# One 6 MB transfer for each expert of a mixture-of-experts layer, and a result that lags by one expert

## The chip, the cores and the metric

The kernel runs on one core of one Trainium2 chip. The metric is device time in microseconds. The time before is the median of three executions.

## The reference, cut to what matters

Two transformer blocks follow one another on 512 tokens of width 1024, all in float32. The change touches only the last part, a hierarchical mixture of 64 experts, of which each token uses two:

```python
# N_EXPERTS = 64, D_MODEL = 1024, D_FF_EXPERT = 512, MOE_TOP_K = 2
def expert_block(args):
    xblk, e = args
    hdn = jax.nn.silu(xblk @ w1[e]) * (xblk @ w3[e])
    return hdn @ w2[e]
...
yb = lax.map(expert_block, (xb, blk_e)).reshape(n_rows, d)
return jnp.zeros_like(xt).at[buf_tok].add(yb * buf_w[:, None])
```

w1 and w3 of an expert are 1024 x 512, w2 is 512 x 1024. Each is 2 MB, so an expert has 6.29 MB of weights and all 64 have 403 MB.

## The kernel before, in words

The first 1400 us compute the attention block, its dense feed-forward layer, the second block's convolution and state-space branches, and the router. The expert stage follows and is the rest of the run.

In that stage every expert gets 64 token rows, however many of them are in use. GpSimd gathers the rows of two experts at once from DRAM (`rows`, L3016 to L3022, 128 rows of 4 KB, of which the unused ones move nothing), and writes each expert's result back with a scatter (`results`, L3024 to L3029, 128 rows of 2 KB). Both use GpSimd's DMA queue, q0. During iterations 3 to 26 GpSimd also issues one small table write each (L3056 to L3059) on the same queue. The gather of pair q is issued at the top of GpSimd's iteration 2q-4, and TensorE uses it at the top of its iteration 2q-2.

The weights come on SyncE's queue, q1, one DMA for each matrix. There are nine slots of 16 KB for each partition (`ring9`, L789), each with its own semaphore. `use_order` (L797 to L804) lists the matrices in the order in which TensorE uses them. The loop at L3136 issues them in that order. Load i waits until TensorE has finished with load i-9, which is known from the PSUM bank of its last matmul: `mh` for w1 and w3, `my` for w2. A line of 16 KB for each partition is contiguous in DRAM. The last w2 comes in four parts, each with a semaphore of its own (`LAST_PARTS`).

TensorE (L1444 to L1462) does in iteration n, in this order:

- for even n `rows`: eight transposes of the next gathered pair (L1405), which VectorE scales and copies to SBUF (L2839);
- `hidden(n)`: w1 and w3 of expert n, in two halves of the array at once (L1418, L1420), 32 matmul instructions in all;
- `turn(n-1)`: four transposes of the hidden values (L1428), after ScalarE has copied them out of PSUM (L1555);
- `result(n-2)`: 16 matmul instructions with w2 (L1441), after ScalarE's silu (L2028) and VectorE's product (L2868). VectorE scales the result (L2876), and the scatter follows.

The result therefore lags by two experts. The PSUM banks are handed out by `bank_table` in the same order. A loop for experts with more than 64 tokens (`over_blocks`) stands behind the stage.

Of the kernel before, what the change touches and what calls it, by code (L numbers as in the profile page):

```python
# [7 lines left out]
F32 = mybir.dt.float32  # L8
# [13 lines left out]
NE = 64  # L22
BLK = 64
OVER = 16
# [31 lines left out]
DMA_SEMS = ["const", "in0", "in1", "in2", "in3", "param", "ol", "c_d", "nck0", "nck1", "w0", "w1", "w2", "w3", "m0", "m1", "m2", "m3", "m4",  # L56
# [10 lines left out]
LAST_PARTS = ["ymix", "x2b", "y01"]  # L67

# [114 lines left out]
def bank_table(ps):  # L183
# [174 lines left out]
    for n in range(NE + 2):  # L358
        if n < NE:
            if n % 2 == 0 and n + 2 < NE:  # L360
                gather(n // 2 + 1)
            if n < NE - 1:
                t("mh", n)
        if 1 <= n <= NE:
            t("mt", n - 1)
        if n == NE - 2:
            t("mh", NE - 1)
        if n >= 2:
            t("my", n - 2)
# [169 lines left out]
def build_program(nc, a):  # L539
    with ExitStack() as ctx:  # L540
# [5 lines left out]
        for name, off, n in [(f"r{off}", off, n) for off, n in PARTS_AT] + [("ring_r", 32768 + 2 * WC, 2 * WC)]:  # L546
            with ExitStack() as under:
                if off:
                    under.enter_context(nc.sbuf_tensor("before_" + name, [128, off], F32))
                parts[name] = under.enter_context(nc.sbuf_tensor(name, [128, n], F32R))  # L550
# [136 lines left out]
        EW = [A[:, 12288 + WC * i:12288 + WC * (i + 1)] for i in range(3)]  # L687
# [101 lines left out]
        ring9 = [(RG[:, i * WC:(i + 1) * WC], sem[f"w{i}"]) for i in range(4)] + [(A[:, 12288 + WC * i:12288 + WC * (i + 1)], sem[f"m{i}"]) for i in range(5)]  # L789
        if len(loads) % 2:  # L790
            ring9[0], ring9[1] = ring9[1], ring9[0]
        ring9 = [ring9[i] for i in (0, 1, 4, 8, 6, 3, 2, 5, 7)]
        before9 = [[ld.value for ld in loads if ld.slot is s] for _, s in ring9]
        before9 = [max(x) if x else 0 for x in before9]


        use_order = []  # L797
        for n in range(NE + 2):
            if n < NE - 1:
                use_order += [("w1", n), ("w3", n)]  # L800
            if n == NE - 2:
                use_order += [("w1", NE - 1), ("w3", NE - 1)]
            if n >= 2:
                use_order.append(("w2", n - 2))  # L804
        turn_of = {key: i for i, key in enumerate(use_order)}

        def matrix(*key):
            i = turn_of[key]
            ap, s = ring9[i % 9]
            return ap, s, before9[i % 9] + 16 * (i // 9 + 1)  # L810
# [24 lines left out]
        def pe(e):  # L835
# [609 lines left out]
            for n in range(NE + 2):  # L1445
                if n == 0:
                    hidden(0)
                if n % 2 == 0 and n + 2 < NE:
                    rows(n // 2 + 1)
                if 0 < n < NE - 1:  # L1450
                    hidden(n)
                if n == 0:
                    u = ps("ov")
                    w.wait_ge(sem["ovl"], 1)
                    w.wait_ge(u.free, u.n)
                    e.matmul(u.ap[0:1, 0:OVER], KEEP[:, 24:25], ident[:, 0:OVER], start=True, stop=True).then_inc(u.full, 1)
                if 1 <= n <= NE:
                    turn(n - 1)
                if n == NE - 2:
                    hidden(NE - 1)  # L1460
                if n >= 2:
                    result(n - 2)  # L1462

            def block(at, done):
                loop_wait(e, osem["gather"], done * 16)
                for k in range(8):
                    m = e.transpose(PS[:, 0, k * BLK:(k + 1) * BLK], OXG[:, k * 128:(k + 1) * 128], C("ident", 0, BLK)[:, 0:BLK])
                m.then_inc(osem["xt"], 1)
                loop_wait(e, osem["xtc"], done)
                loop_wait(e, osem["load"], done * 96)  # L1470
                for k in range(8):
                    e.matmul(PS[0:64, 1, :], OXT[:, k, :], cols(EW[0], 8)[:, k, :], start=k == 0, stop=k == 7)
                    m = e.matmul(PS[64:128, 1, :], OXT[:, k, :], cols(EW[1], 8)[:, k, :], start=k == 0, stop=k == 7)
                m.then_inc(osem["h"], 1)
                loop_wait(e, osem["hc"], done)
                for j in range(4):
                    m = e.transpose(PS[:, 2, j * 128:(j + 1) * 128], H13[0][:, j * 128:(j + 1) * 128], ident)
                m.then_inc(osem["ht"], 1)
                loop_wait(e, osem["mul"], done)
                for k in range(4):  # L1480
                    for hh in range(2):
                        m = e.matmul(PS[64 * hh:64 * hh + 64, 3, :], HT[0][:, k, :], cols(EW[2], 4)[:, k, 512 * hh:512 * hh + 512], start=k == 0, stop=k == 3)
                m.then_inc(osem["y"], 1)
# [44 lines left out]
        def act(e):  # L1528
# [501 lines left out]
            for n in range(NE + 1):  # L2030
                if n == 2:
# [6 lines left out]
                if n < NE:  # L2038
                    if n >= 2:
                        ut = ps("mt", n - 2)  # L2040
                        w.wait_ge(ut.full, ut.n + 1)
                    u = ps("mh", n)
                    evict(H13[n % 2].rearrange("t (k p) -> t p k", k=4), u, ACT.Copy, src=u.ap.rearrange("t (p k) -> t p k", k=4))
                if n >= 1:
                    gate_half(n - 1)
# [27 lines left out]
        def dve(e):  # L2073
# [787 lines left out]
            for n in range(NE + 2):  # L2861
                if n < NE and n % 2 == 0 and n + 2 < NE:
                    rows(n // 2 + 1)
                if 1 <= n <= NE:
                    ex = n - 1
                    u = ps("mt", ex)
                    w.wait_ge(sem["sl"], ex + 1)
                    e.tensor_tensor(HT[ex % 2], SL[ex % 2], cols(u.ap, 4)[:, :, 64:128], ALU.mult).then_inc(u.free, 1)  # L2868
                if n >= 2:
                    ex = n - 2  # L2870
                    u = ps("my", ex)
                    if ex >= 2:
                        w.wait_ge(sem[f"yo{ex % 2}"], 16 * (ex // 2))
                    w.wait_ge(sem["g2b"], 32)
                    w.wait_ge(u.full, u.n + 1)
                    e.tensor_tensor(YO[ex % 2], u.ap, G2, ALU.mult).then_inc(u.free, 1)  # L2876
# [36 lines left out]
        def pool(e):  # L2913
# [134 lines left out]
            for n in range(NE + 2):  # L3048
# [5 lines left out]
                if n >= 2:  # L3054
                    results(n - 2)
# [5 lines left out]
            def block(at, done):  # L3061
                loop_wait(e, osem["load"], done * 96)
# [8 lines left out]
        def sp(e):  # L3071
# [64 lines left out]
            for i, (what, ex) in enumerate(use_order):  # L3136
                ap, s, _ = matrix(what, ex)
# [3 lines left out]
                elif i < 9:  # L3141

                    u = ps("so" if i < 5 else "mo", 7)
                    w.wait_ge(u.full, u.n + 1)
                    if i == 4:
# [8 lines left out]
                src = a[what][ex].rearrange("(p k) n -> p k n", p=128)  # L3154
                if (what, ex) == ("w2", NE - 1):
                    for k in range(4):
                        e.dma_start(cols(ap, 4)[:, k, :], src[:, k, :]).then_inc(sem[LAST_PARTS[k - 1]] if k else s, 16)
                else:
                    e.dma_start(cols(ap, 4 if what == "w2" else 8), src).then_inc(s, 16)  # L3159

            def block(at, done):
                loop_wait(e, osem["next"], done)
                ex = e.value_load(OVI[0:1, bass.ds(at, 1)], min_val=0, max_val=NE - 1)
                for i, (name, k) in enumerate((("w1", 8), ("w3", 8), ("w2", 4))):
                    src = a[name].rearrange("x (p k) n -> x p k n", p=128)[bass.ds(ex, 1)].rearrange("x p k n -> (x p) k n")
                    e.dma_start(cols(EW[i], k), src).then_inc(osem["load"], 16)
# [91 lines left out]
def arrays(x):  # L3258
# [8 lines left out]
        "w_mix_out": x["w_mix_out_2"][0], "w1": x["w1_2"][0], "w3": x["w3_2"][0], "w2": x["w2_2"][0],  # L3267
# [23 lines left out]
```

## Time and profile before

| | |
|---|---|
| median of 3 runs | 2425.97 us (2423.55 to 2429.41) |
| span of the profiled execution | 2425.2 us |
| time of the profiled execution around its span | not given by the page; its span is 0.8 us under the median |
| TensorE busy | 2267.0 us, 93% of the span |
| DMA in the last 16 of 40 slices | 9 tenths busy or more until the last slice, 412 to 427 GB/s |
| all DMA | 598.76 MB in 175417 packets |
| queue q1 (SyncE) | 564.39 MB |
| queue q0 (GpSimd) | 8.46 MB in 10592 packets |

Each of the 40 slices of the page is 60.6 us long. The expert stage fills the last 17 of them. A TensorE that is shown as busy may still be waiting for the DMA queues in short gaps, so the stage is read from the waits and from the DMA share, not from TensorE's busy time. GB/s is what all 16 DMA engines moved together; the queue lines of the profile give each queue's packets, its bytes, and the time of its packets as a share of the time of all 16 engines.

### The profile page before, as it was taken

How to read it: one execution, taken by the hardware profiler on the slowest of the kernel's cores; microseconds unless marked ns; L12 is line 12 of the kernel's file. 1: busy time of each engine (PE TensorE's matmuls, PEld its weight loads, DVE VectorE, ACT ScalarE, POOL GpSimd, SP SyncE). 2: the span in 40 equal slices, each digit the busy share in tenths (PEclk: the TensorE clock that was granted, in tenths of full speed). 3: DMA queues.
4: the chain of work that ended last, by engine and by line, in shares of the span. 5: the costliest groups of instructions: out<-in, count | busy, mean ns of one | idle time of the engine just before them, and what ended most of it. 6: DMA issues, size and time to landing. Idle time of an engine off the chain costs nothing. (4 is left out here: it accounts for less than half of the span.)

```text
span 2425.2 us, 26229 instructions
## 1 busy us (share of the span) xinstructions
PE 2267.0 (93%) x10596; PEld 1416.4 (58%) x10596; DVE 1048.8 (43%) x1730; ACT 718.5 (30%) x1163; POOL 783.4 (32%) x491
## 2 busy tenths in 40 slices
PE   8999999999999999999999999888888888888887
PEld 6676578888887787777777873222222222322233
DVE  6666654443456999746765233111111111211112
ACT  5435643222233333557674221000000000000001
POOL 3335655545553443433336521111111011101000
PEclk9999999999999999999999999999999999999999
DMA  4222243534545243253345269999999999999996
GB/s 161 99 101 68 96 140 113 200 134 162 190 122 139 71 104 109 75 170 120 131 153 205 104 269 412 425 422 424 424 425 425 426 426 425 427 425 426 427 426 272
DMA packets 175417, 598.76 MB, mean 247 GB/s; under 512 B 18098, under 2 KB 96946, under 8 KB 149696
## 3 DMA queue, kind: packets, MB, share of 16 engines
q1 hardware_dynamic: 156000, 564.39, 59.8%
q10 hardware_dynamic: 8704, 24.22, 2.6%
q0 software_dynamic: 10592, 8.46, 1.1%
q8 instruction: 85, 1.39, 0.3%
q14 instruction: 36, 0.29, 0.0%
HBM read 593.19 MB, written 28.97 MB: 257 GB/s over the span
## 5 line engine op out<-in xcount | busy, mean ns | idle before, releaser
L2923 POOL TENSOR_TENSOR ring_r<-ring,ring_r 128x1024 fp32r<-128x1024 f32 (+2 forms) x215 | 513.3, 2393 | 650.2 <-ACT ring_r L1544 650.0
L857 PE MATMUL ps<-r,ring_r 128*128 128x512 f32 x1512 | 605.3, 400 | 3.8 <-POOL ring_r L2923 1.5
L859 PE MATMUL ps<-r,ring_r 128*128 128x512 f32 x1512 | 590.5, 391 | 0.0
L858 PE MATMUL ps<-r,ring_r 128*128 128x512 f32 x1512 | 590.1, 390 | 0.0
L1555 ACT ACTIVATE arena<-ps 128x512 f32<-128x512 f32 (+4 forms) x200 | 150.5, 761 | 1046.8 <-PE ps L1420 852.8
L1420 PE MATMUL ps<-arena 128*64 128x512 f32 x672 | 317.9, 629 | 68.7 <-DMA arena<-in_w 68.5
L1418 PE MATMUL ps<-arena 128*64 128x512 f32 x672 | 328.8, 639 | 0.9 <-DMA arena<-in_w 0.9
L1544 ACT ACTIVATE ring_r<-ring 128x1024 fp32r<-128x1024 f32 x220 | 222.8, 1015 | 351.9 <-PE ps L859 192.1
L857 PEld LDWEIGHTS ps<-r,ring_r 128*128 128x128 f32 x1512 | 282.9, 187 | 75.3 <-issue 10.5
L3028 POOL DMA_INDIRECT y_d<-arena,cbm x64 | 63.7, 995 | 805.0 <-DVE arena L2876 539.6
L858 PEld LDWEIGHTS ps<-r,ring_r 128*128 128x128 f32 x1512 | 282.9, 187 | 64.3 <-issue 5.8
L859 PEld LDWEIGHTS ps<-r,ring_r 128*128 128x128 f32 x1512 | 282.7, 187 | 62.5
L2868 DVE TENSOR_TENSOR arena<-arena,ps 128x256 f32<-128x256 f32 x64 | 27.0, 421 | 613.6 <-ACT arena L2028 613.6
L1420 PEld LDWEIGHTS ps<-arena 128*64 128x64 f32 x672 | 93.4, 144 | 249.3 <-issue 150.0
L1420 PE MATMUL ps<-ring,arena 128*64 128x512 f32 x352 | 169.1, 637 | 43.7 <-DMA ring<-in_w 43.7
L1418 PE MATMUL ps<-ring,arena 128*64 128x512 f32 x352 | 166.6, 621 | 1.1 <-DVE arena L2839 1.1
L1441 PE MATMUL ps<-ring,arena 128*64 128x512 f32 x672 | 153.5, 599 | 0.0
L2480 DVE SCALAR_TENSOR_TENSOR ps<-arena,params_sb,ps 128x512 f32<-128x512 f32 x232 | 153.1, 749 | 0.0
L1420 PEld LDWEIGHTS ps<-ring,arena 128*64 128x64 f32 x352 | 49.7, 146 | 141.5 <-issue 82.2
L1418 PEld LDWEIGHTS ps<-arena 128*64 128x64 f32 x672 | 93.4, 146 | 44.6 <-issue 39.6
L2876 DVE TENSOR_TENSOR arena<-ps,scr 128x512 f32<-128x512 f32 x64 | 44.3, 691 | 170.9 <-PE ps L1441 167.1
L1441 PEld LDWEIGHTS ps<-ring,arena 128*64 128x64 f32 x672 | 44.5, 137 | 79.0 <-issue 79.0
(377 smaller groups left out, 2550.8 us busy)
## 6 DMA issues: line engine op xcount, KB each, us to landing
arena<-in_w SPq DMA_DIRECT2D x105, 2048.0 KB, 33.7
ring<-in_w SPq DMA_DIRECT2D x86, 2048.0 KB, 37.0
ring<-in_w_ada SPq DMA_DIRECT2D x12, 2048.0 KB, 7.9
ring<-in_ffn_w_in SPq DMA_DIRECT2D x22, 1024.0 KB, 7.6
ring<-in_w_in SPq DMA_DIRECT2D x40, 512.0 KB, 6.2
ring<-in_w_in SPq DMA_DIRECT2D x8, 2048.0 KB, 9.3
ring<-in_fox_w_in SPq DMA_DIRECT2D x7, 2048.0 KB, 8.4
arena<-acs_d SPq DMA_DIRECT2D x16, 512.0 KB, 3.6
```

What stands on the lines that cost most here:

```text
L857: e.matmul(out, wh[:, k, :], X.hi[:, k0 + k, :], start=first and k == 0, stop=False)
L858: e.matmul(out, wh[:, k, :], X.lo[:, k0 + k, :], start=False, stop=False)
L859: m = e.matmul(out, wl[:, k, :], X.hi[:, k0 + k, :], start=False, stop=last and k == nk - 1)
L1418: e.matmul(u.ap[0:64], x, cols(w1, 8)[:, k, :], start=k == 0, stop=k == 7)
L1420: m = e.matmul(u.ap[64:128], x, cols(w3, 8)[:, k, :], start=k == 0, stop=k == 7)
L1441: m = e.matmul(u.ap[64 * hh:64 * hh + 64], HT[ex % 2][:, k, :], cols(w2, 4)[:, k, 512 * hh:512 * hh + 512], start=k == 0, stop=k == 3)
L1544: e.activation(GH[t], raw, ACT.Copy).then_inc(sem["gr_hi"], 1)
L1555: return e.activation(dst, u.ap if src is None else src, func, **how).then_inc(u.free, 1)
L2480: m = e.scalar_tensor_tensor(acc if i < 30 else cv[:, nt, :], u_rows[:, nt, i:i + T], PR[:, w0:w0 + 1], acc, ALU.mult, ALU.add)
L2876: e.tensor_tensor(YO[ex % 2], u.ap, G2, ALU.mult).then_inc(u.free, 1)
L2923: e.tensor_tensor(GL[t], grans[t][1], GH[t].bitcast(F32), ALU.subtract).then_inc(sem["gr_lo"], 1)
L3028: e.indirect_dma_start(a["y_d"], bass.IndirectOffsetOnAxis(ap=YROW[:, ex:ex + 1], axis=0), YO[ex % 2], None, bounds_check=4 * T - 1, oob_i ...
```

## The change

The host lays w2, w1 and w3 of an expert side by side, so that a partition's 48 KB are one contiguous line in DRAM. SBUF has three slots of 48 KB for each partition in place of nine of 16 KB, at the same addresses. Experts 9 to 60 come in one DMA of 6 MB. The load of expert n waits for `my` of expert n-3, that is, for the whole slot. The first nine matrices come singly, experts 3 to 8 and 61 to 63 come as w1 with w3 (32 KB lines) and w2 (16 KB lines).

The result of expert n-1 now stands between `hidden(n)` and `turn(n)`. ScalarE's, VectorE's and GpSimd's loops are moved by one iteration to match, and the last steps stand in a list.

```diff
+SLOT_OF = (1, 0, 2)
+PARTED = 9
+LAST_STEPS = [("mh", NE - 2), ("mt", NE - 2), ("mh", NE - 1), ("my", NE - 3), ("mt", NE - 1), ("my", NE - 2), ("my", NE - 1)]
...
+        first = [("w3", 0), ("w2", 2)]
+        for what, n in (first[::-1] if len(loads) % 2 else first) + [("w1", 0), ("w3", 1), ("w2", 1), ("w1", 1), ("w2", 0), ("w1", 2), ("w3", 2)]:
+            expert_load(n, what)
+        for n in range(3, PARTED):
+            expert_load(n, "w1", "w3")
+            if n > 3:
+                expert_load(n - 1, "w2")
+        expert_load(PARTED - 1, "w2")
+        for n in range(PARTED, NE - 3):
+            expert_load(n, "w2", "w1", "w3")
+        for n in range(NE - 3, NE):
+            expert_load(n, "w1", "w3")
+        for n in range(NE - 3, NE):
+            expert_load(n, "w2")
...
             rows(0)
-            for n in range(NE + 2):
-                if n == 0:
-                    hidden(0)
-                if n % 2 == 0 and n + 2 < NE:
+            hidden(0)
+            rows(1)
...
+            turn(0)
+            for n in range(1, NE - 2):
+                if n % 2 == 0:
                     rows(n // 2 + 1)
-                if 0 < n < NE - 1:
-                    hidden(n)
...
-                if 1 <= n <= NE:
-                    turn(n - 1)
-                if n == NE - 2:
-                    hidden(NE - 1)
-                if n >= 2:
-                    result(n - 2)
+                hidden(n)
+                result(n - 1)
+                turn(n)
+            for what, n in LAST_STEPS:
+                {"mh": hidden, "mt": turn, "my": result}[what](n)
...
                 else:
-                    kind, old = use_order[i - 9]
-                    u = ps("my" if kind == "w2" else "mh", old)
+
+                    u = ps("my" if "w2" in whats else "mh", ex - 3)
                     w.wait_ge(u.full, u.n + 1)
...
-                    e.dma_start(cols(ap, 4 if what == "w2" else 8), src).then_inc(s, 16)
+                    e.dma_start(dst, src).then_inc(done, 16)
```

The loop for overfull experts now fetches its three matrices in one DMA as well.

## Rows read from the trace of the kernel before

**Rows 1.** The page: DMA total, then the chain that ended last, by engine.

```profile
DMA packets 175417, 598.76 MB, mean 247 GB/s; under 512 B 18098, under 2 KB 96946, under 8 KB 149696
...
DMA 28%; PE 11%; issue 0%; DVE 0%; SPq 0%; ACT 0%; ACTq 0%; POOLq 0%; DVEq 0%
```

**Rows 2.** Busy time by stretch: length, PE, PEld, DVE, ACT, POOL, PEclk, DMA share, GB/s.

```profile
1450.00:1460.00 10.00, 8.40 (x43) 3.80 (x44) 8.14 (x35) 0.19 (x1) 0.99 (x1) 1.00 0.93 356
...
2000.00:2100.00 100.00, 86.08 (x373) 29.77 (x371) 16.89 (x45) 7.76 (x13) 11.14 (x11) 0.97 1.01 425
```

**Rows 3.** DMA, 2000 to 2300 us: share of 16 engines; issues, median us to landing.

```profile
DMA packets 11668, 127.74 MB, mean 426 GB/s; under 512 B 3302, under 2 KB 3302, under 8 KB 3998
...
q1 hardware_dynamic: 8616, 125.47, 98.4%
q0 software_dynamic: 3040, 2.10, 2.2%
...
y_d<-arena,cbm POOLq DMA_INDIRECT x20, 7.8
arena<-n_d,cbm POOLq DMA_INDIRECT x10, 11.9
```

**Rows 4.** DMA, 1600 to 2300 us: queue q0 and what was issued on it.

```profile
q0 software_dynamic: 7504, 5.78, 2.5%
...
y_d<-arena,cbm POOLq DMA_INDIRECT x46, 7.8
arena<-n_d,cbm POOLq DMA_INDIRECT x23, 12.0
row_d<-cbm POOLq DMA_INDIRECT x16, 7.8
```

**Rows 5.** DMA issues, 1447.4 to 1451 us: gathers while q1 stands empty.

```profile
arena<-n_d,cbm POOLq DMA_INDIRECT x2, 3.2
```

**Rows 6.** DMA issues, 2355 to 2400 us: scatters at the end.

```profile
y_d<-arena,cbm POOLq DMA_INDIRECT x5, 3.6
```

**Rows 7.** Queue q1, 600 to 700 us: packets, MB, share of 16 engines.

```profile
q1 hardware_dynamic: 13292, 16.58, 49.1%
```

**Rows 8.** Queue q1, 2389.8 to 2394.4 us.

```profile
q1 hardware_dynamic: 78, 0.27, 14.6%
```

**Rows 9.** Timeline of TensorE, two experts: start, us, line, shape, count [idle before].

```profile
1896.08 1.12 PE L1420 MATMUL ps<-arena 128*64 128x512 f32 x1 [3.21 <-DMA arena<-in_w]
...
1906.04 0.66 PE L1428 MATMUL ps<-consts_sb,arena 128*128 128x128 f32 x4
1906.62 3.66 PE L1441 MATMUL ps<-arena 128*64 128x512 f32 x16
1910.21 1.09 PE L1405 MATMUL ps<-consts_sb,arena 128*128 128x128 f32 x8
1911.23 0.64 PE L1418 MATMUL ps<-arena 128*64 128x512 f32 x1
...
1918.25 0.66 PE L1428 MATMUL ps<-consts_sb,arena 128*128 128x128 f32 x4
1918.84 3.65 PE L1441 MATMUL ps<-ring,arena 128*64 128x512 f32 x16
```

**Rows 10.** Timeline of SyncE: a load issued into an empty q1.

```profile
1403.60 0.34 SPq L3159 DMA_DIRECT2D ring<-in_w  x1
```

**Rows 11.** Busy time by stretch, the 0.9 us behind that issue.

```profile
1403.60:1404.50 0.90, 0.90 (x5) 0.74 (x5) 0.00 (x0) 0.00 (x0) 0.00 (x0) 1.00 0.00 0
```

**Rows 12.** Timeline of GpSimd: the gather behind a result's scatter.

```profile
1913.15 1.04 POOL L3021 DMA_INDIRECT arena<-n_d,cbm  x1 [0.30 <-issue]
```

**Rows 13.** Timeline of TensorE at the end: the last `hidden` and the last `result`.

```profile
2374.37 1.07 PE L1418 MATMUL ps<-ring,arena 128*64 128x512 f32 x2
...
2393.81 3.60 PE L1441 MATMUL ps<-arena 128*64 128x512 f32 x16
```

**Rows 14.** DMA issues of SyncE, 2357.6 to 2400 us: the last w2's four parts.

```profile
arena<-in_w SPq DMA_DIRECT2D x4, 512.0 KB, 34.6
```

More of the change, by code:

```diff
@@ L357, in bank_table @@
     gather(0)
-    for n in range(NE + 2):
-        if n < NE:
-            if n % 2 == 0 and n + 2 < NE:
-                gather(n // 2 + 1)
-            if n < NE - 1:
-                t("mh", n)
-        if 1 <= n <= NE:
-            t("mt", n - 1)
-        if n == NE - 2:
-            t("mh", NE - 1)
-        if n >= 2:
-            t("my", n - 2)
+    for n in range(NE - 2):
+        if n % 2 == 0:
+            gather(n // 2 + 1)
+        t("mh", n)
+        if n >= 1:
+            t("my", n - 1)
+        t("mt", n)
+    for what, n in LAST_STEPS:
+        t(what, n)
     for tt in range(4):
@@ L545, in build_program @@
         parts = {}
-        for name, off, n in [(f"r{off}", off, n) for off, n in PARTS_AT] + [("ring_r", 32768 + 2 * WC, 2 * WC)]:
+        for name, off, n in [(f"r{off}", off, n) for off, n in PARTS_AT] + [("ring_r", 32768 + 2 * WC, 2 * WC), *((f"expert{i}", 12288 + 3 * WC * i, 3 * WC) for i in range(3))]:
             with ExitStack() as under:
@@ L549, in build_program @@
                     under.enter_context(nc.sbuf_tensor("before_" + name, [128, off], F32))
-                parts[name] = under.enter_context(nc.sbuf_tensor(name, [128, n], F32R))
+                parts[name] = under.enter_context(nc.sbuf_tensor(name, [128, n], F32 if name.startswith("expert") else F32R))
         A = ctx.enter_context(nc.sbuf_tensor("arena", [128, 32768], F32))
@@ L787, in pv_done @@
             return sem["pv"], m + 1 - (m + 1) // 4
[L789 to L810, printed above, removed]
+        EX = [parts[f"expert{i}"][:, :] for i in range(3)]
@@ new lines, in build_program, with expert_load @@
+        AT = {"w2": 0, "w1": WC, "w3": 2 * WC}
+        EW2, EW1, EW3 = (EX[0][:, WC * i:WC * (i + 1)] for i in range(3))
+        expert_loads, landed, signalled = [], {}, {}
+        def expert_load(n, *whats):
+            slot = SLOT_OF[n % 3]
+            lo, hi = AT[whats[0]], AT[whats[-1]] + WC
+            name = f"xa{slot}" if whats == ("w2",) else f"xb{slot}"
+            signalled[name] = signalled.get(name, 0) + 16
+            for what in (whats if whats == ("w2",) else {*whats, "w1", "w3"}):
+                landed[what, n] = sem[name], signalled[name]
+            expert_loads.append((n, whats, EX[slot][:, lo:hi], a["wx"][n][:, lo:hi], sem[name]))
@@ L812, in build_program, with matrix @@
+        for n in range(NE - 3, NE):
+            expert_load(n, "w2")
+        def matrix(what, n):
+            return EX[SLOT_OF[n % 3]][:, AT[what]:AT[what] + WC], *landed[what, n]
         XR = Split(rawH, rawL, lambda k: lows["raw", k])
@@ L1444, in pe @@
             rows(0)
-            for n in range(NE + 2):
-                if n == 0:
-                    hidden(0)
-                if n % 2 == 0 and n + 2 < NE:
-                    rows(n // 2 + 1)
-                if 0 < n < NE - 1:
-                    hidden(n)
[L1452 to L1457, printed above, removed]
-                    turn(n - 1)
-                if n == NE - 2:
-                    hidden(NE - 1)
-                if n >= 2:
-                    result(n - 2)
+            hidden(0)
+            rows(1)
+            u = ps("ov")
+            w.wait_ge(sem["ovl"], 1)
+            w.wait_ge(u.free, u.n)
+            e.matmul(u.ap[0:1, 0:OVER], KEEP[:, 24:25], ident[:, 0:OVER], start=True, stop=True).then_inc(u.full, 1)
+            turn(0)
+            for n in range(1, NE - 2):
+                if n % 2 == 0:
+                    rows(n // 2 + 1)
+                hidden(n)
+                result(n - 1)
+                turn(n)
+            for what, n in LAST_STEPS:
+                {"mh": hidden, "mt": turn, "my": result}[what](n)
             def block(at, done):
@@ L1469, in block @@
                 loop_wait(e, osem["xtc"], done)
-                loop_wait(e, osem["load"], done * 96)
+                loop_wait(e, osem["load"], done * 64)
                 for k in range(8):
-                    e.matmul(PS[0:64, 1, :], OXT[:, k, :], cols(EW[0], 8)[:, k, :], start=k == 0, stop=k == 7)
-                    m = e.matmul(PS[64:128, 1, :], OXT[:, k, :], cols(EW[1], 8)[:, k, :], start=k == 0, stop=k == 7)
+                    e.matmul(PS[0:64, 1, :], OXT[:, k, :], cols(EW1, 8)[:, k, :], start=k == 0, stop=k == 7)
+                    m = e.matmul(PS[64:128, 1, :], OXT[:, k, :], cols(EW3, 8)[:, k, :], start=k == 0, stop=k == 7)
                 m.then_inc(osem["h"], 1)
@@ L1481, in block @@
                     for hh in range(2):
-                        m = e.matmul(PS[64 * hh:64 * hh + 64, 3, :], HT[0][:, k, :], cols(EW[2], 4)[:, k, 512 * hh:512 * hh + 512], start=k == 0, stop=k == 3)
+                        m = e.matmul(PS[64 * hh:64 * hh + 64, 3, :], HT[0][:, k, :], cols(EW2, 4)[:, k, 512 * hh:512 * hh + 512], start=k == 0, stop=k == 3)
                 m.then_inc(osem["y"], 1)
@@ L2028, in gate_half @@
                 e.activation(SL[ex % 2], cols(u.ap, 4)[:, :, 0:64], ACT.Silu).then_inc(sem["sl"], 1)
-            for n in range(NE + 1):
-                if n == 2:
+            for n in range(NE):
+                if n == 1:
                     for i in range(2):
@@ L2860, in dve, with gated, scaled @@
             e.tensor_tensor(GATE0, cols(ident, 1).broadcast_to([128, 4, 128]), WK[0].broadcast_to([128, 4, 128]), ALU.mult).then_inc(sem["wk"], 1)
-            for n in range(NE + 2):
-                if n < NE and n % 2 == 0 and n + 2 < NE:
-                    rows(n // 2 + 1)
[L2864 to L2876, printed above, removed]
+            def gated(ex):
+                u = ps("mt", ex)
+                w.wait_ge(sem["sl"], ex + 1)
+                e.tensor_tensor(HT[ex % 2], SL[ex % 2], cols(u.ap, 4)[:, :, 64:128], ALU.mult).then_inc(u.free, 1)
+            def scaled(ex):
+                u = ps("my", ex)
+                if ex >= 2:
+                    w.wait_ge(sem[f"yo{ex % 2}"], 16 * (ex // 2))
+                w.wait_ge(sem["g2b"], 32)
+                w.wait_ge(u.full, u.n + 1)
+                e.tensor_tensor(YO[ex % 2], u.ap, G2, ALU.mult).then_inc(u.free, 1)
+            for n in range(NE - 2):
+                if n % 2 == 0:
+                    rows(n // 2 + 1)
+                if n >= 1:
+                    scaled(n - 1)
+                gated(n)
+            for what, n in LAST_STEPS:
+                if what == "mt":
+                    gated(n)
+                elif what == "my":
+                    scaled(n)
             def block(at, done):
@@ L3047, in pool @@
             rows(1)
-            for n in range(NE + 2):
+            for n in range(NE + 1):
                 if n % 2 == 0 and n + 4 < NE:
@@ L3053, in pool @@
                     w.wait_ge(sem["slot"], 6)
-                if n >= 2:
-                    results(n - 2)
+                if n >= 1:
+                    results(n - 1)
                 if 3 <= n < 27:
@@ L3134, in sp @@
                     spread(p)
-            for i, (what, ex) in enumerate(use_order):
-                ap, s, _ = matrix(what, ex)
+            for i, (ex, whats, dst, src, done) in enumerate(expert_loads):
                 if i < 2:
```

32 lines of the change are left out of this document (13 added, 19 removed).

## The prediction

> **What bounds the kernel now.** I read the page's chain first: 28% of the span is DMA and 11% TensorE [rows 1]. The DMA part consists of long pieces of expert weights, so only the expert stage can give or cost much. Busy time by stretch says how full the DMA engines are there: share 1.01 and 425 GB/s from 2000 to 2100 us, with TensorE at 86 of 100 us [rows 2]. The stage is bound by bytes through full DMA engines. The queue lines give its step. q1 moves 125.47 MB in 300 us [rows 3], or 418 GB/s, so an expert's 6.29 MB take 15.04 us. Of the 11668 packets 3998 are under 8 KB, which leaves 7670 that carry 125.47 MB, 16.4 KB each: one packet for each partition's line. TensorE has slack. Behind `hidden` at 1911.23 come `turn` at 1918.25 and `result` until 1922.49 [rows 9], 11.26 us for an odd expert and 1.0 us more (L1405) for an even one, 23.5 us in a pair of 30.1.
>
> **1. Larger packets.** For one expert each of the 16 DMA engines handles 24 data packets and 3 completions now, and 8 and 1 with whole loads. That is 18 fewer. What does a packet cost beyond its bytes? q1 in [rows 3]: 0.984 x 16 x 300 us / 8616 = 548 ns at 14562 bytes. In [rows 8]: 0.146 x 16 x 4.6 / 78 = 138 ns at 3460 bytes. The line through both is 37 ns per 1000 bytes plus 9.8 ns. With [rows 7], 785.6 us / 13292 = 59 ns at 1247 bytes, it has 13.3 ns. But in the full stage the queues' shares add up to 100.8%, so packets overlap by 0.8% of 548 ns, 4.4 ns each. I take 9.8 - 4.4 = 5.4 ns. 18 x 5.4 ns x 52 whole experts = 5.1 us. The 9 experts in two loads save 9 packets each, 0.4 us. Term: -5.5 us. Bounds: 0 (lines cut up as before) and -13 us (13.3 ns with no overlap). No trace here shows a packet over 16 KB.
>
> **2. Three slots, a load released by `my` of n-3.** Let T be the landing of expert n. `hidden(n)` and `result(n-1)` take 11.26 - 0.59 (the `turn` that now comes later) = 10.7 us. Then SyncE issues load n+2; an issue into an empty queue moves nothing for 0.9 us [rows 10, 11]. First packet: T + 11.7. The engines are busy with load n+1 until T + 15.0, less what lies between a last packet and the matmul that waits for it, which no row shows (0 to 1 us). The queue stays full with 2.3 to 3.3 us to spare. The cover is thin where the clock falls. After 3.21 us of idle time `hidden` took 1896.08 to 1906.04, 9.96 us against 7.02 [rows 9]; this stretch has a mean granted clock of 0.97 [rows 2]. TensorE's idle time before an odd expert will be 15.04 - 11.26 = 3.8 us and before an even one 2.7, so the odd ones may well start at 1.2 GHz and use 2.9 us of the cover. Each then ends between 0.4 us early and 0.6 us late. For 26 such experts: 0 to +16 us. I take +2.5, since the nearer end is no wait.
>
> **3. `result` ahead of `turn`.** No instruction is added; both wait on results that are long there. `result(n-1)` needs the product of `turn(n-1)` in the step before. `turn(n)` now has ScalarE's copy (L1555) hidden behind `result(n-1)`'s 3.6 us. VectorE, ScalarE and GpSimd are idle most of the stage [rows 2]. Cost 0. PSUM: eight banks for on average four uses an expert, as before.
>
> **4. Start.** The first nine loads are again 18.9 MB, singly, behind the same waits. From 1450 on the engines are at 0.93 and above [rows 2]. Loads of experts 3 to 8 keep the old rule (w1 and w3 wait for `mh`), and TensorE, at 11.8 us an expert, is then ahead of the queue, with `my(6)` some 5 us before the load of expert 8 ends. 0 us, bounds -1 and +3.
>
> **5. End.** Now `hidden(63)` starts at 2374.37 and the last result ends at 2397.4, 23.0 us later, with four loads of w2 behind w3(63) in the queue. The last part lands at about 2357.6 + 34.6 + 2 = 2394 to 2395 [rows 13, 14], so TensorE runs on 2.5 us after it. After the change three w2 (15 us) follow, and 7.0 + 3 x 3.6 + 0.6 = 18.4 us of TensorE work: at least 3.4 us behind the last landing, 5 if a cold `hidden(61)` makes the chain late. +0.5 to +2.5, I take +1.3. The loop for overfull experts did not run and costs nothing.
>
> **Sum.** 2425.2 - 5.5 + 2.5 + 1.3 = 2423.5 us of span. The median of the runs lies 0.8 us above the span of the profile: 2424.3.
>
> **A cost on another queue.** The scatter takes 7.8 us to land in the full stage [rows 3] and 3.6 with q1 running out [rows 6]; the gather 12.0 [rows 4] and 3.2 with q1 empty [rows 5]. In the 300 us there are 20 scatters, 10 gathers and 3040 q0 packets. That is 16 x (20 x 5 + 10 x 9): 5 and 9 packets on each engine. With 46, 23 and 16 table writes of 2, it is 16 x 469 = 7504, as [rows 4] have it. A gather stands behind its scatter, 14 packets; (12.0 - 3.2) / 14 = 0.63 us each, one 16 KB packet of q1. So the engines alternate between the queues, packet by packet. With 48 KB packets every q0 packet waits some 1.85 us. In two experts q1 then offers 16 data packets and 2 completions, 18 turns, and q0 wants 19 (23 in iterations up to 26, with the table writes).
>
> The Trainium skill bears on this (DMA: Bandwidth & Descriptors, Queues, rings and completion order): an engine round-robins between its queues and drains a whole packet, typically 9 to 17 descriptors, before it switches. The alternation agrees. The size doesn't: by that rule a turn of q1 would be an engine's whole share of a 2 MB load, 4.9 us, and five turns 24 us, where a loaded scatter lands in 7.8. Its advice to coalesce transfers would by its fixed 2 us a DMA save 4 us an expert if nothing overlapped; a DMA share of 1.01 excludes that.
>
> **Rivals.**
> *B, slower: the gathers come late behind 48 KB packets.* A gather will take 3.2 + 14 x 1.85 = 29.1 us, with a table write in front 32.8. It is issued 2.9 us after its `result` (ends 1910.27, issue 1913.15 [rows 9, 12]), at T + 13.6 of odd expert n-1, 1.3 later with a table write, 2.9 later if that expert was cold. TensorE wants it at the latest 1.1 us ahead of the landing of n+2, at T + 44.0. Allowed: 27.5 to 30.4 us against 29.1, and with table writes 26.2 to 29.1 against 32.8, before any backlog. There it is late by 3.7 to 6.6 us; part 2's cover takes 0.4 to 3.3. The first dry moment of q1 lets q0 empty itself, so I let every second of the 9 table pairs pay 2.4 us, +11 us, and the later pairs nothing. 2435. It decides only when the lateness exceeds the cover; if all 9 paid in full it would be +50. For it: the turns, counted exactly. Against: only the slowest engine must keep q1 full; on engines that are ahead q0 drains freely, and small waits of part 2 drain it too.
> *C, faster: a packet's cost is not overlapped.* 18 x 9.8 ns x 52 + 0.7 = 9.9 us saved, no late issue, +0.5 at the end: 2425.2 - 9.9 + 0.5 + 0.8 = 2416.6. Against: the shares above 100%.
> *D, nothing larger moves: 48 KB lines go as three packets.* No saving, no slower q0; 2425.2 + 2.5 + 1.3 + 0.8 = 2430, or 2427 without late issues. Every line of 16 KB so far went as one packet, which speaks against it.
>
> **Chances.** A (the sum) 0.35, B 0.32, C 0.25, D 0.08. What a measurement of this kernel can tell from no change is 0.2%, 4.9 us: below 2421.1 is faster, above 2430.8 slower. A's own range is 2419 to 2430, so a little of it is faster. Faster 0.29 (C and 0.04 of A), same 0.40 (A's rest, D, a mild B), slower 0.31. Range: 2414 takes in C, nearly to the bound of part 1; 2441 takes in B with six pairs paying 3 us. A's own range is as above.
>
> **What would show it.** Packets of 48 KB in the queue lines (over 8 KB, a third as many): else D. q1 at 420 GB/s or more with share 1.01 between 1900 and 2300: part 1; the step from 15.04 to about 14.95 us. Scatters landing in 13 us or more and gathers in about 29: the turns. TensorE idle before L1405 for a DMA on n_d, with the DMA share below 1 between 1565 and 1830 us: B. Dips spread evenly with a lower granted clock: part 2. The sum is wrong if the share falls below 0.99 anywhere from 1500 to 2370, or if gathers keep to 12 us although packets are 48 KB.

## The result, and the profile after

The changed kernel takes 2452.47 us (median of four runs, 2451.15 to 2454.1), the kernel before 2427.31 beside it on the same chip: a ratio of 1.011, interval 1.0097 to 1.0122. It is slower by 1.1%, 28 us above the forecast and 11 above the range. The profiled execution spans 2451.4 us, 26.2 more than before. Times and ratios below come with runs of the kernel before on the same chip.

The page of the changed kernel: the DMA total, then the chain by engine, to be held against [rows 1], and the GB/s of the 40 slices of 61.3 us each.

```profile
GB/s 164 94 100 79 83 139 138 179 158 145 192 125 112 103 87 95 121 136 121 126 137 233 101 341 418 418 408 401 414 415 392 406 418 412 396 413 421 409 425 294
DMA packets 159145, 598.75 MB, mean 244 GB/s; under 512 B 16290, under 2 KB 95138, under 8 KB 147888
...
DMA 25%; PE 15%; issue 1%; DVE 0%; ACT 0%; POOL 0%; ACTq 0%; POOLq 0%; SPq 0%; DVEq 0%
```

The bytes are the same, the packets 16272 fewer. Nothing is lost up to slice 25. Then no slice of the expert stage but the last full one reaches 425, and in the chain TensorE has 4 points more and DMA 3 fewer. In a stage that was bound by a full queue this points at loads that wait for TensorE.

Busy time by stretch of the changed kernel (columns as in [rows 2]).

```profile
1500.00:1565.00 65.00, 58.10 (x284) 21.49 (x284) 13.32 (x34) 7.29 (x10) 14.28 (x15) 1.00 1.01 428
1565.00:1830.00 265.00, 202.48 (x900) 71.53 (x902) 38.43 (x96) 23.27 (x32) 40.09 (x40) 0.91 0.98 409
1830.00:2000.00 170.00, 140.67 (x613) 48.91 (x610) 24.61 (x61) 15.62 (x21) 17.13 (x17) 0.90 0.97 402
2000.00:2300.00 300.00, 242.12 (x1072) 85.01 (x1072) 47.46 (x120) 28.02 (x39) 30.30 (x30) 0.90 0.99 412
```

And the kernel before.

```profile
1565.00:1830.00 265.00, 231.78 (x990) 79.07 (x988) 42.27 (x107) 23.04 (x36) 43.04 (x43) 0.95 1.01 424
1830.00:2000.00 170.00, 147.84 (x628) 50.04 (x624) 25.66 (x64) 14.07 (x22) 17.18 (x17) 0.95 1.01 426
2000.00:2300.00 300.00, 259.19 (x1103) 88.15 (x1102) 46.64 (x119) 25.58 (x40) 30.38 (x30) 0.96 1.01 426
```

The loss is everywhere from the first whole loads on, with the table writes (to 1830) and without them, and with it the granted clock falls from 0.95 to 0.90. Before the first whole load is waited for (1500 to 1565) the changed kernel is the faster one, 428 against 423.

Queue q1 from 1565 to 2300 us (packets, MB, share of 16 engines), first of the kernel before, then of the changed one.

```profile
q1 hardware_dynamic: 21030, 306.31, 98.2%
```

```profile
q1 hardware_dynamic: 6737, 294.18, 95.4%
```

In 735 us the changed kernel moves 12.13 MB of weights less; at 416.7 GB/s, the rate before, that is 29.1 us. The rest of the kernel gives 3 us back, so this stretch is the whole of the loss. An expert's 6.29 MB took 15.1 us and now take 15.7.

DMA of the changed kernel, 2000 to 2300 us, beside [rows 3].

```profile
DMA packets 5680, 123.60 MB, mean 412 GB/s; under 512 B 2529, under 2 KB 2529, under 8 KB 3199
...
q1 hardware_dynamic: 2778, 121.36, 96.2%
q0 software_dynamic: 2890, 2.07, 2.1%
...
expert<-in_wx SPq DMA_DIRECT2D x19, 6144.0 KB, 19.3
y_d<-arena,cbm POOLq DMA_INDIRECT x20, 16.6
arena<-n_d,cbm POOLq DMA_INDIRECT x10, 28.5
```

5680 - 3199 = 2481 packets carry 121.36 MB, 48.9 KB each: the long lines do go as one packet. The scatter takes 16.6 us where it took 7.8, the gather 28.5 where it took 11.9; 29.1 had been forecast. Most telling is the first issue line. A load lands 19.3 us after its issue. A step, from one landing to the next, takes 14.9 us where it is shortest, so the load stands in the queue only some 4 us before its turn comes.

What TensorE waits for from 1600 to 2300 us (total, times, longest), first before, then after.

```profile
PE ps L1420 <- DMA arena<-in_w: 60.6, 22, 3.4
PE ps L1420 <- DMA ring<-in_w: 31.1, 12, 4.2
```

```profile
PE ps L1430 <- DMA expert<-in_wx: 129.2, 42, 6.2
PE ps L1417 <- DMA arena<-n_d,cbm: 8.8, 6, 3.8
```

The waits for weights grow from 91.7 to 129.2 us. Those for the gathers, rival B, are 8.8. (The total alone proves little: one experiment below has 117.4 us of them and no loss.)

Timeline of TensorE in the changed kernel, three experts (start, us, line, count, idle before). L1430 is `hidden`, L1453 `result`.

```profile
2063.22 0.64 PE L1430 MATMUL ps<-expert,arena 128*64 128x512 f32 x1 [0.57 <-DMA expert<-in_wx]
...
2070.14 3.60 PE L1453 MATMUL ps<-expert,arena 128*64 128x512 f32 x16
...
2079.84 1.12 PE L1430 MATMUL ps<-expert,arena 128*64 128x512 f32 x1 [5.51 <-DMA expert<-in_wx]
...
2088.57 3.60 PE L1453 MATMUL ps<-expert,arena 128*64 128x512 f32 x16
...
2094.73 0.64 PE L1430 MATMUL ps<-expert,arena 128*64 128x512 f32 x1 [0.85 <-DMA expert<-in_wx]
...
2111.59 1.12 PE L1430 MATMUL ps<-expert,arena 128*64 128x512 f32 x1 [5.75 <-DMA expert<-in_wx]
```

SyncE's loads in the same stretch.

```profile
2073.78 0.33 SPq L3172 DMA_DIRECT2D expert<-in_wx  x1
...
2092.21 0.33 SPq L3172 DMA_DIRECT2D expert<-in_wx  x1
```

Read the two together. The expert that landed at 2063.22 starts warm (0.64 us for its first matmul), `hidden` and `result` are through by 2073.7, and the load is issued 10.6 us after the landing and 6.1 before the next one at 2079.84. It lands 14.9 us after that one, at 2094.73: a full step. The expert that landed at 2079.84 comes after 5.51 us of idle time and starts at half the clock (1.12 us). Its `hidden` takes 8.7 us instead of 6.9, its load goes out 12.4 us after the landing and only 2.5 before 2094.73, and lands 16.9 after it, at 2111.59. That expert again finds TensorE idle for 5.75 us and slow.

The rest of the stage is less regular, but has the same two sides. From 1600 to 2300 us 18 of 45 experts start at the half clock (a first matmul of 1.1 us). Call the time from a load's issue to the landing of the load ahead of it the cover: 19 of the 51 loads that follow a whole load have less than 3 us, 15 have 5 us or more. Their mean steps are 16.2 and 15.1 us.

### The profile page after: what moved, and what is told of

Read it like the earlier page. It is cut to its first block and busy times, and to the rows that moved or that the text cites. A ratio compares the mean times of both kernels' runs of the same rounds, so it can differ in the third digit from the quotient of the medians.

```text
span 2451.4 us, 26113 instructions
## 1 busy us (share of the span) xinstructions
PE 2235.0 (91%) x10596; PEld 1410.0 (58%) x10596; DVE 1049.3 (43%) x1730; ACT 729.5 (30%) x1163; POOL 786.7 (32%) x491
## 5 line engine op out<-in xcount | busy, mean ns | idle before, releaser
L1430 PE MATMUL ps<-expert,arena 128*64 128x512 f32 x1024 | 510.9, 657 | 159.8 <-DMA expert<-in_wx 158.7
L1432 PE MATMUL ps<-expert,arena 128*64 128x512 f32 x1024 | 510.9, 657 | 0.0
L1430 PEld LDWEIGHTS ps<-expert,arena 128*64 128x64 f32 x1024 | 148.4, 151 | 474.5 <-issue 303.9
L1453 PE MATMUL ps<-expert,arena 128*64 128x512 f32 x1024 | 230.5, 592 | 1.2 <-DVE arena L2871 1.2
L1453 PEld LDWEIGHTS ps<-expert,arena 128*64 128x64 f32 x1024 | 73.1, 137 | 147.6 <-issue 147.6
L1432 PEld LDWEIGHTS ps<-expert,arena 128*64 128x64 f32 x1024 | 148.4, 151 | 0.0
L2846 DVE TENSOR_SCALAR arena<-ps,params_sb 128x128 f32<-128x128 f32 x256 | 84.5, 406 | 15.0 <-PE ps L1417 14.9
L2949 POOL TENSOR_TENSOR r<-arena,r 128x512 fp32r<-128x512 f32 x53 | 72.6, 1377 | 47.4 <-ACT r L1712 15.6
L2037 ACT ACTIVATE arena<-ps 128x256 f32<-128x256 f32 x64 | 24.6, 384 | 188.4 <-PE ps L1440 188.4
L2091 DVE RECIPROCAL scr<-scr 128x528 f32<-128x528 f32 (+1 forms) x16 | 54.4, 3402 | 42.5 <-ACT scr L1564 42.5
```

The lines of the kernel that those rows point to most:

```text
L1430: e.matmul(u.ap[0:64], x, cols(w1, 8)[:, k, :], start=k == 0, stop=k == 7)
L1432: m = e.matmul(u.ap[64:128], x, cols(w3, 8)[:, k, :], start=k == 0, stop=k == 7)
L1453: m = e.matmul(u.ap[64 * hh:64 * hh + 64], HT[ex % 2][:, k, :], cols(w2, 4)[:, k, 512 * hh:512 * hh + 512], start=k == 0, stop=k == 3)
L2846: m = e.tensor_scalar(XT[i][:, k, :], u.ap[:, 128 * j:128 * j + 128], SC2[:, k:k + 1], SH2[:, k:k + 1], ALU.mult, ALU.add)
L2949: e.tensor_tensor(dst, src, hi.bitcast(F32), ALU.subtract).then_inc(done, 1)
```

## The experiments

The theory after the result, M: loads are released too late, above all behind a slow `hidden`, and q1 runs dry for a moment. Its rival is B, the gathers that stand behind long packets. "Whole" below is a load of one expert in one DMA.

**Shorter packets, same waits.**

```diff
-                    e.dma_start(dst, src).then_inc(done, 16)
+                    for k in range(3):
+                        e.dma_start(dst[:, WC*k:WC*k+WC], src[...]).then_inc(done, 16)
```

> The changed kernel, but each whole load goes out as three DMAs of 16 KB lines, issued together behind the same wait. Two theories of the 26 us. Theory M (late release): a slot is released by the result two experts later, 10.7 us after a landing where TensorE's clock is high and some 13.5 us where it is low, and then the DMA queue runs dry for a moment. M expects no recovery: 2445 to 2456 us, and expert steps that alternate between 14.9 and 16.5 us as in the changed kernel. Theory B (48 KB packets make the gathers and scatters of the other queue late): the packets are 16 KB again, gathers land in 12 to 15 us, and the time goes back to 2425 to 2432 us.

Measured: 2464.63 us against 2424.45, ratio 1.0157 (1.0136 to 1.0178). Its DMA issues and TensorE's wait, 1600 to 2300 us.

```profile
y_d<-arena,cbm POOLq DMA_INDIRECT x44, 8.1
arena<-n_d,cbm POOLq DMA_INDIRECT x22, 12.2
```

```profile
PE ps L1430 <- DMA expert<-in_wx: 146.8, 40, 7.2
```

The gathers are as quick as before the change, TensorE waits for none, and the kernel is slower still. So B isn't what costs here. That it is 12 us slower than the change itself was not expected. Some 6 of them are the gain of the long lines, which is gone; and from 1565 to 2300 us the 16 engines stand idle for 24.2 us where it was 17.4 in the changed kernel. Why they idle longer is not shown.

**The same lines, released in two.** w1 with w3 waits for `mh` of n-3, w2 for its `my`, for every expert.

```diff
-PARTED = 9
+PARTED = 61
```

> The changed kernel, but all experts from 3 on come as experts 3 to 8 do: w1 with w3 (32 KB lines) released by the hidden step of n-3, and w2 (16 KB lines) by the result of n-3. Theory M (the whole slot is released too late to keep the queue full) expects most of the 26 us back, since two thirds of the bytes are asked for 18 us earlier: 2422 to 2434 us and steps of 15.0 us. A theory by which 48 KB packets or the larger unit are harmful in themselves expects 2430 to 2440 us, since the 32 KB packets keep half of it.

Measured over ten runs: 2425.7 us against 2425.52, ratio 1.0001 (0.9991 to 1.001). Its q1 from 1565 to 2300 us.

```profile
q1 hardware_dynamic: 14094, 307.47, 97.9%
```

Its busy time from 1600 to 2300 us, and TensorE's wait.

```profile
1600.00:2300.00 700.00, 584.30 (x2592) 206.10 (x2594) 109.97 (x276) 66.97 (x92) 86.83 (x87) 0.91 1.01 428
```

```profile
PE ps L1430 <- DMA expert<-in_wx: 117.4, 45, 5.5
```

The order of the results, the slots and the late `turn` are those of the change; the packets are 16 and 32 KB. The 32 KB now enter the queue some 18 us earlier (the 4 MB loads take 37.5 us from issue to landing, the whole ones took 19.3), and the loss is gone. With 16 KB packets and the late release it was not, so it is the release that decides. The low clock is still there: 0.91, and 17 of 47 experts start at the half clock, after 4.1 us of idle time on average. So late loads are not needed for slow experts, and slow experts cost nothing while the queue is full.

**TensorE kept busy.** Three matmuls ahead of each `turn` of experts 8 to 57, some 2.7 us of work whose products nobody reads.

```diff
+                for j in range(3 if 8 <= ex < NE - 6 else 0):
+                    e.matmul(u.ap[0:64], ident[:, 0:64], cols(w1, 8)[:, j, :], start=True, stop=True)
```

> The changed kernel with three matmuls more (2.6 us, result not used) ahead of the turn of experts 8 to 57, behind the matmul that releases a slot, so that TensorE idles about 1.2 us ahead of an odd expert and not 3.8. If the low clock is what makes the releases late, every release comes 10.7 us after a landing, the alternation of 14.9 and 16.5 us steps ends and the kernel gets faster although it does more: 2428 to 2440 us. If the cover is too thin even at the high clock, or the other queue is the cause, 2448 to 2458 us.

Measured: 2433.98 us, ratio 1.0038 (1.0022 to 1.0053). Busy time from 1600 to 2300 us, then TensorE's wait.

```profile
1600.00:2300.00 700.00, 653.91 (x2852) 232.58 (x2850) 110.14 (x276) 67.00 (x92) 86.42 (x86) 0.99 1.00 422
```

```profile
PE ps L1430 <- DMA expert<-in_wx: 43.5, 41, 2.1
```

The same stretch of the changed kernel.

```profile
1600.00:2300.00 700.00, 561.88 (x2476) 197.12 (x2474) 106.83 (x266) 64.39 (x89) 84.51 (x84) 0.91 0.98 409
```

TensorE is busy for 92 us more and the kernel is 18 us faster, with the packets and the rule of release unchanged and gathers at 27.9 us. Only one of 46 experts starts at the lower of the two clock levels (1.2 and 2.4 GHz), and only 4 of 51 loads have a cover under 3 us, where it was 19. So some 18 of the 25 us are paid through the clock, which makes releases late. The 8 to 9 us that are left fit a cover that is still thin: 36 of the 51 loads have 4 to 5 us of it, and their mean step is 15.2 us.

**No table writes.** They and the wait for them are left out, for experts 3 to 26.

```diff
-                if 3 <= n < 27:
-                    i, at = divmod(n - 3, 8)
...
-            w.wait_ge(sem["scat"], 16 * 24)
```

> The changed kernel without the 24 small table writes of iterations 3 to 26 on GpSimd's queue (they serve only experts with over 64 tokens, of which there are none with these inputs). B expects that the other queue then wants 19 turns for two experts and not 23, so that the loss between experts 10 and 27, 12 us in the changed kernel, halves: 2443 to 2448 us. M expects within 3 us of the changed kernel's 2452.

Measured: 2449.98 us, ratio 1.0108 (1.0084 to 1.0132). Not to be told from the change. B's worst stretch, with 23 turns for q0 against 18, isn't where the time goes.

**No lag.** `hidden`, `turn` and `result` of one expert in a row. Loads should go out one step earlier, but the gather's time runs out.

```diff
-                hidden(n)
-                result(n - 1)
-                turn(n)
+                hidden(n)
+                turn(n)
+                result(n)
```

> 48 KB lines as in the changed kernel, but the order hidden(n), turn(n), result(n) up to expert 60: the slot of n is released 13.5 us after its landing and not after that of n+1, so the load of n+3 is issued some 16 us before the queue needs it. M expects that the queue never runs dry: 15.0 us a step or a little less, and 2418 to 2428 us in all. B expects that the late gathers remain and are worse, as nothing lets the other queue empty itself: 2440 to 2470 us, with TensorE waiting for gathers.

Measured: 2467.96 us, ratio 1.0168 (1.0142 to 1.0193). What TensorE waits for from 1600 to 2300 us, and gathers from 2000 to 2300.

```profile
PE ps L1416 <- DMA arena<-n_d,cbm: 56.1, 12, 7.7
```

```profile
arena<-n_d,cbm POOLq DMA_INDIRECT x10, 27.4
```

Here B is real: the gathers take what they take in the changed kernel, but TensorE wants them sooner and waits 4.7 us each time, and for no weights. TensorE then runs late itself and so do its releases: the loads land 20.4 us after their issue, hardly more than the 19.3 of the changed kernel. The 16 us of cover that were expected are not there.

The same with each load as three DMAs of 16 KB lines.

> Lag zero as in e5, with three DMAs of 16 KB lines for each load. In e5 TensorE never waited for weights but 64 us for gathers that took 27 us to land. Theory B (48 KB packets make the gathers late) expects gathers of 12 us again, no wait for them, a full queue, and 2425 to 2440 us (a slow start and end of some 10 us stay). If e5 was slow for its order of steps alone, 2455 to 2470 us.

Measured: 2434.99 us, ratio 1.0043 (1.0027 to 1.006). The gathers over the same 300 us.

```profile
arena<-n_d,cbm POOLq DMA_INDIRECT x10, 11.9
```

With short packets the wait for the gathers is gone and some 30 us with it. The very edit that cost 12 us behind the late release saves 30 where the gather is what is waited for: which packet is better depends on what ends last.

**Rows asked for later.** The gather one iteration later, lag 1 to expert 10 and then none.

```diff
+    for n in range(1, NE - 3):
+        if n % 2 == 1 and n > 1:
+            out.append(("mx", (n + 1) // 2))          # rows; they stood at even n, two experts ahead
...
+        out.append(("mh", n))
...
+        elif n == early:                              # 10
+            out += [("my", n - 1), ("mt", n), ("my", n)]
+        else:
+            out += [("mt", n), ("my", n)]
```

> 48 KB lines; lag of one expert up to expert 10 and of zero after it, and TensorE uses a gathered pair one iteration later (at 2q-1 and not 2q-2), which allows a gather 15 us more. With both causes removed (late release, late gathers) and large packets kept, the DMA engines should stay full at 14.95 us an expert: 2417 to 2430 us. If 48 KB packets cost something else in a full queue, above 2435 us.

Measured: 2444.09 us, ratio 1.0087 (1.0065 to 1.0108). Two stretches, then what TensorE and VectorE wait for, 1600 to 2300 us.

```profile
1800.00:1900.00 100.00, 78.56 (x356) 28.41 (x356) 15.32 (x39) 8.53 (x12) 14.02 (x14) 0.93 0.93 392
1900.00:2000.00 100.00, 80.79 (x358) 27.91 (x354) 16.39 (x43) 9.41 (x13) 10.12 (x10) 0.93 1.01 432
```

```profile
PE ps L1434 <- DMA arena<-n_d,cbm: 37.6, 11, 8.9
...
DVE arena L2889 <- DMA y_d<-arena,cbm: 268.3, 24, 21.2
```

Whole loads in a full queue move up to 432 GB/s, where the kernel before has 427 in the same 100 us. From 2000 to 2300 us this kernel's q1 carries 126.47 MB.

```profile
q1 hardware_dynamic: 2893, 126.47, 98.0%
```

Against the 125.47 MB of [rows 3] that is a step of 14.92 us for 15.04. In that stretch gathers take 41.2 us and scatters 29.3, and around 1850 us, where they bind, the rate falls to 392. B is the price of a full queue of 48 KB packets. That in the changed kernel the dry moments let q0 through, as the forecast held against B, fits its 28.5 us but was not tested.

**Every second expert in two.** If only one parity is late, parting that one should mend all. First the odd ones in two.

```diff
+            if n % 2 == 0:
                 expert_load(n, "w2", "w1", "w3")
+            else:
+                expert_load(n, "w1", "w3")
+                expert_load(n, "w2")
```

> Of experts 9 to 60 only the even ones come in one 6 MB load; the odd ones come as w1 with w3 (released by the hidden step of n-3) and w2. In the changed kernel it is the loads of odd experts that are released by a step at the low clock. If the late release at the low clock is the cause of the 26 us, it is cured here with half of the 48 KB lines kept, and the other queue gets 27 turns for two experts, over the 23 that it wants: steps of 14.95 us and 2419 to 2427 us, at or a little below the kernel before. If whole loads cost by their size, half of the loss remains: 2435 to 2441 us.

> The control for e9: the odd experts come in one 6 MB load and the even ones in two. Bytes, packets and turns are the same as in e9. If a late release at the low clock is the cause, the loads that it hits stay whole and part of the loss stays: 2430 to 2445 us, 8 us or more above e9. If size or number of the packets decides, the same time as e9 within 3 us.

Measured: 2458.05 us, ratio 1.0129 (1.0109 to 1.0149), for odd ones in two; 2449.64, 1.01 (1.0087 to 1.0114), for even ones. Both miss, and the control is the faster one. TensorE's wait with odd ones in two, 1600 to 2300 us.

```profile
PE ps L1434 <- DMA expert<-in_wx: 143.5, 22, 7.5
```

22 waits of 6.5 us, before the experts whose load is whole. The slow clock is not tied to a parity, it goes where the whole loads are, and those still go out late: at 2018.90 us, 3.0 us before the landing ahead at 2021.86. And SyncE issues in order: the part that stands behind it, whose slot was free one `result` sooner, goes out at 2019.28.

**Both at once.** The order of "rows later", and odd experts from 9 in two; then fewer of them in two (from expert 28 on each fourth).

```diff
+            if n % 2:                                 # second kernel: n % 2 if n < 28 else n % 4 == 1
+                expert_load(n, "w1", "w3")
+                expert_load(n, "w2")
```

> Both causes removed and half of the 48 KB lines kept: the order of e6 (lag zero from expert 11, gathered pairs used one iteration later), and odd experts from 9 to 60 come as w1 with w3 and w2, so that q1 offers 27 turns for two experts where the other queue wants 19 to 23. e6 lost its time in bursts of gathers that landed after 41 us; if that is all that stood in the way, gathers land in about 20 us, the queue stays full at 14.9 us an expert and the kernel takes 2416 to 2424 us, below both. If lag zero or the rest of the order costs by itself, 2430 us or more.

> As e12, but from expert 28 on, where the table writes are over, only every fourth expert comes in two: 45 turns for four experts where the other queue wants 38. If turns are what counts, the queue stays full here too and the time is 0 to 2 us below that of e12. If the gathers get late again for another reason, 5 us or more above e12.

Measured: 2425.14 us, ratio 0.9993 (0.9984 to 1.0002), eleven runs; 2425.07, 0.9995 (0.9986 to 1.0004), eleven runs. The first one's stretch from 1600 to 2300 us, and its gather.

```profile
1600.00:2300.00 700.00, 577.56 (x2614) 205.07 (x2610) 110.94 (x278) 66.82 (x94) 89.60 (x89) 0.96 1.00 427
```

```profile
arena<-n_d,cbm POOLq DMA_INDIRECT x10, 21.6
```

The first misses its forecast of 2416 to 2424 us; the second is not to be told from the first. Two quite different repairs (each load in two with an early part; no lag, later rows and half the loads in two) both bring the loss to nothing, and neither beats the kernel before by more than its interval.

## Why the prediction was wrong, step by step

**1. Larger packets: right, small.** Packets of 48.9 KB exist. In a full queue they take 14.92 us an expert for 15.04 (rows asked for later, 2000 to 2300 us), so some 6 us over 52 experts were to be had, as the term of -5.5 has it. The kernel released in two shows it: 307.47 MB in q1 from 1565 to 2300 against 306.31, 2.8 us. It lost 3.4 us between 1450 and 1500 (368 GB/s against 396), for which I have no cause.

**2. The release: the step that failed.** It gave `hidden` and `result` 10.7 us and a cold one 2.9 more; measured are 10.6 and 12.4. It gave a cold expert's first packet between 0.4 us early and 0.6 late, and took +2.5, with a bound of +16. Measured: the 29.1 us of the stretch and the gain of 5 to 6 that they swallowed, some +34 to +35. What failed is the reckoning of when the queue is dry. A load issued 12.4 us after the landing should send its first packet 0.6 to 1.6 us before that; yet it landed 16.9 us after the load ahead, 2 us late. The traces have each load's issue and landing. Here they are for the five kernels in which experts 9 to 60 come in one DMA each (the changed kernel, TensorE kept busy, no table writes, no lag, rows asked for later).

| cover of a whole load | loads | mean step |
|---|---|---|
| under 2 us | 25 | 17.7 us |
| 2 to 3 us | 31 | 16.0 us |
| 3 to 4 us | 14 | 15.6 us |
| 4 to 5 us | 73 | 15.3 us |
| 5 us and more | 112 | 14.9 us |

The forecast has nothing lost down to a cover of 0.9 to 1.9 us; in these runs a cover under some 5 us costs. The cold expert's cover was 2.5 us.

The packets of the changed kernel say why. The term "0 to 1 us" between a last packet and the matmul is 2.0 us: that long before the landing the last sixteen packets of a load, about one for each engine, end on average. The first sixteen of a load issued with under 3 us of cover start on average 1.3 us after the issue, the very first after 0.96. So an average engine needs 3.3 us and not 0.9 to 1.9.

And the first packet behind a dry moment is slow, of which the prediction had nothing: 5.6% of the 5985 long packets from 1565 to 2300 us take over 1.25 times the usual 1815 ns, and 303 of these 336 are among the first sixteen of their load (0.7 us over the usual with a cover under 3 us, none from 5 us up). Over the stretch the excess of the slow packets is 17.1 us of all 16 engines' time, and engines stand idle for 17.4 us of it (0.0 before the change). The price is thus half gap and half slow start, 34.5 us together, which is the +34 to +35.

The other half of the step held: TensorE's idle time before every second expert was put at 3.8 us, with a slow expert behind it; 18 of 45 are slow, here after up to 6.2 us of idle time and in the kernel released in two, with no load late, after 4.1. Late loads lengthen that idle time, but whether this makes more experts slow is not shown: the kernel released in two has about as many. The extra matmuls thicken the cover and win back 18 us.

The Trainium skill (DMA: Bandwidth & Descriptors, Queues, rings and completion order) has an engine drain a whole packet of its queue, typically 9 to 17 descriptors, before it turns to the next queue. The measured turns are shorter, one line of 16 or 48 KB each, since gathers take 11.9 and 28.5 us as 14 turns of one line give them.

**3. `result` ahead of `turn`: right.** Nobody waits for it; the kernel released in two has the same order and loses nothing.

**4. Start: right in sum.** 399 and 428 GB/s from 1450 to 1565 against 396 and 423 before.

**5. End: the term right, another one missed.** +1.3 was forecast for TensorE running on behind the last landing. It ran on 2.6 us before (2394.8 to 2397.4) and 4.5 after (2419.5 to 2424.0), +1.9. The rate by slices shows what was missed. The GB/s of 2300 to 2425 us before, in 40 slices of 3.1 us.

```profile
GB/s 425 419 431 431 421 426 425 425 425 440 419 435 425 425 425 425 432 424 430 419 425 435 425 419 438 406 367 313 157 79 7 34 37 333 405 387 212 168 240 263
```

And of 2300 to 2450 us after, in slices of 3.75 us.

```profile
GB/s 437 446 339 400 419 425 421 433 439 422 435 340 428 464 419 403 445 463 420 359 425 436 424 446 414 447 428 397 428 410 401 161 10 46 124 400 389 258 227 260
```

Before, the last loads peter out over four slices (367, 313, 157, 79), 5.8 us of full rate not used; after, over one (161), 2.3 us. That gives 3.5 us back. With 1.1 us from the start, 29.1 - 3.5 - 1.1 + 1.9 is 26.4 of the 26.2 us of span.

**The rivals.** B's mechanism was right to the turn (gather 29.1 us forecast, 28.5 measured; scatter "13 us or more", 16.6) and its price of 11 us wrong: TensorE waits 8.8 us for gathers, and shorter packets give no time back. Its condition, a full q1, isn't met in the changed kernel; where TensorE wants its rows sooner (no lag) or q1 is kept full (rows later), B decides. C needs a step of 14.86 us, and 14.92 is the best that a full 300 us show; D fell. The signs named for part 2, dips spread evenly with a lower granted clock, and a DMA share under 0.99, are what the profile shows. The chances went wrong because no rival stood for part 2 at its full size: its price was capped at 16 us, and that by a term, 0 to 1 us, that no row showed.

## What to carry to other kernels

- Before joining transfers, ask what releases each: one load waits for the last reader of all its parts. A queue that was full through early, small releases then lives on the margin of the latest one, and here that turned a gain of 5 us into a loss of 25. Join the lines if you like, but part the waits.
- A queue is not full until its last byte has landed. The engines finish their shares at different times, so measure in the trace how long before a landing the next load must be issued for the step to stay short, before you call a margin enough.
- Where an engine idles before each transfer and then starts at the lower clock, take the release at that clock. It costs nothing while the queue is full and most of the loss when the cover is thin.
- Longer packets on one queue lengthen small transfers on another; count their turns, and see what waits for them.

## What the runs showed of the hardware

- A queue that is refilled shortly before it runs out still loses time: over 255 loads of 6 MB in five kernels, the mean step is 14.9 us with 5 us or more between the issue and the landing ahead, 15.3 with 4 to 5, 16.0 with 2 to 3 and 17.7 with less than 2.
- The first packet on each engine behind a dry moment is slow: 0.7 us above the usual 1.8 for 48 KB.
- Queues take turns line by line: a gather lands in 3.2 us alone, 11.9 to 12.2 beside 16 KB packets, 16.2 beside 16 and 32 KB, 28.5 beside 48 KB in a queue that runs dry, and 41.2 in one kept full.
- TensorE's clock stood at the half after 5.5 us of idle time, and useless matmuls (126 us of them between 1600 and 2300 us) raised the granted clock there from 0.91 to 0.99 and made a kernel 18 us faster.
